# A hybrid decoder step on one Trainium2 core: w_o by halves with the sample tile first, and late experts placed on the chip

## What is computed

```python
h = x + merge_out(y_conv, y_nsa, gates, w_o)        # (g_a * y_conv + g_b * y_nsa) @ w_o
xf = rms_norm(h, g_ffn)
lg = xf @ w_rg + b_rg                               # 4 groups
le = (xf @ w_re + b_re).reshape(-1, 4, 8)           # 8 experts in each
g_star = argmax(lg); top_v, top_i = top_k(le[g_star], 2)
w_tok = softmax(top_v) * softmax(lg)[g_star]
eid = g_star * 8 + top_i
y = sum over the two experts of w_tok * (silu(xf @ w_gate[e]) * (xf @ w_up[e])) @ w_down[e]
out = rms_norm(h + y, g_final)
```

## Time and profile before

| what | us |
|---|---|
| median of 3 runs (821.12 to 822.25) | 821.67 |
| the profiled execution | 821.36 |
| its span | 819.5 |
| PE busy in the span | 772.4 (94%) |
| DVE / ACT / POOL busy | 371.3 / 199.9 / 170.7 |

### The profile page before, as it was taken

One profiled execution on the slowest core, in us unless ns is written; L12 is line 12 of the kernel. 1 busy time (PEld: TensorE's weight loads), 2 busy tenths in 40 slices (PEclk: granted clock), 3 DMA queues, 4 the chain that ended last, 5 costly groups with the idle time before them and its releaser, 6 DMA issues.

```text
span 819.5 us, 11726 instructions
## 1 busy us (share of the span) xinstructions
PE 772.4 (94%) x4589; PEld 540.2 (66%) x4589; DVE 371.3 (45%) x790; ACT 199.9 (24%) x435; POOL 170.7 (21%) x270
## 2 busy tenths in 40 slices
PE   5999999999999989999999999999999999998674
PEld 3657778878666667777767777774457855655431
DVE  2201999895488869103026632232137522232106
ACT  3000112131456651215226530000010112222114
POOL 2338548030000015000025220001000212232100
PEclk9999999999999999999999999999998999999878
DMA  9785545178000016521135359508007789999746
GB/s 310 173 30 189 157 104 149 45 218 281 2 1 2 1 32 177 180 77 52 51 85 162 117 148 319 215 1 290 31 26 286 283 325 412 408 403 386 310 158 242
DMA packets 91922, 140.05 MB, mean 171 GB/s; under 512 B 29909, under 2 KB 64881, under 8 KB 90703
## 3 DMA queue, kind: packets, MB, share of 16 engines
q1 hardware_dynamic: 75855, 102.46, 36.8%
q0 software_dynamic: 11392, 32.71, 13.8%
q10 hardware_dynamic: 4616, 4.08, 1.6%
HBM read 133.04 MB, written 21.14 MB: 188 GB/s over the span
## 4 chain that ended last, share of the span: by engine, by line
PE 85%; DVE 6%; DMA 5%; SPq 1%; issue 1%; ACT 1%; ACTq 0%; DVEq 0%; POOL 0%; POOLq 0%
PE ps L1925 18%; PE ps L2117 15%; PE ps L2457 7%; PE ps L2379 7%; PE ps L1949 5%; PE ps L2025 4%; PE ps L2473 3%; DMA arena<-w_up 2%; PE ps L2160 2%; PE ps L2135 2%; PE ps L2148 2%; PE ps L2447 2%; PE ps L2407 2%; DMA arena<-yscratch 2%; PE ps L2221 1%; PE ps L2003 1%
## 5 line engine op out<-in xcount | busy, mean ns | idle before, releaser
L2117 PE MATMUL ps<-xT,keep 128*128 128x288 f32 x512 | 126.9, 407 | 0.8 <-ACT h L1226 0.5
L2117 PEld LDWEIGHTS ps<-xT,keep 128*128 128x128 f32 x512 | 96.5, 190 | 27.4 <-ACT h L1226 0.9
L1925 PE MATMUL ps<-xT,arena 128*128 128x288 f32 x384 | 95.6, 408 | 1.1 <-DVE keep L1508 1.1
L1925 PEld LDWEIGHTS ps<-xT,arena 128*128 128x128 f32 x384 | 72.1, 190 | 20.7 <-issue 1.4
L1415 DVE SCALAR_TENSOR_TENSOR cv<-keep,cv 128x512 f32<-128x512 f32 x120 | 83.6, 746 | 1.4
L2379 PE MATMUL ps<-arena,xT 128*128 128x512 f32 x128 | 55.4, 592 | 0.0
L1000 POOL TENSOR_SCALAR keep<-keep,pmod 128x64 f32<-128x64 f32 x16 | 7.8, 508 | 176.2 <-PE ps L2160 120.0
L2379 PEld LDWEIGHTS ps<-arena,xT 128*128 128x128 f32 x128 | 24.2, 190 | 29.3 <-issue 29.2
L2457 PE MATMUL ps<-keep,mgT 128*64 128x256 f32 x224 | 41.7, 389 | 1.7 <-DMA mgT<-w_up 1.5
L1949 PE MATMUL ps<-mgT,xT 128*128 128x512 f32 (+1 forms) x128 | 43.3, 497 | 0.0
L1045 POOL DMA_INDIRECT yscratch<-cv,slots_of x19 | 19.0, 1001 | 100.2 <-PE ps L2447 67.2
(11 more groups left out here) (411 smaller groups left out, 1331.9 us busy)
## 6 DMA issues: line engine op xcount, KB each, us to landing
arena<-w_down SPq DMA_DIRECT2D x19, 512.0 KB, 16.2
keep<-w_in SPq DMA_DIRECT2D x16, 512.0 KB, 3.9
arena<-w_gate SPq DMA_DIRECT2D x15, 512.0 KB, 7.8
arena<-w_up SPq DMA_DIRECT2D x15, 512.0 KB, 10.8
keep<-w_gate SPq DMA_DIRECT2D x14, 512.0 KB, 10.1
keep<-w_up SPq DMA_DIRECT2D x14, 512.0 KB, 17.5
h<-x_prompt SPq DMA_DIRECT2D x8, 512.0 KB, 5.7
arena<-w_in SPq DMA_DIRECT2D x8, 512.0 KB, 8.7
```

The lines of the kernel that those rows point to most:

```text
L1925: last = mm(tokens(j)[:, b, :], weights(k), halves(x[:, k, :])[:, b, :], start=k == 0, stop=k == n_k - 1)
L2117: last = mm(out[:, 0:half], wmg[n // 2 % 3][:, k, :], xT[:, k, (n % 2) * half:(n % 2 + 1) * half], start=k == 0, stop=k == KD - 1, skip_gr ...
```

## The change

**w_o and router.** `w_o` is loaded as two halves of 512 output columns. The sample tile comes first, then the first half of the columns for tiles 0 to 3 (`wa`), then the second half (`wb`), tile by tile, with turn and logits of the tile before between its products. PE turns `h` itself, not the scaled tile; the scale is applied to the logits on DVE. ACT now writes the scaled tile to `xs2`. Fills are changed in number. When the first halves are done SP loads gate and up of positions 3 and 4; positions 7 and 8 now wait for the first two gathers.

**Late experts.** Positions from 11 on are no longer experts 11 to 31 in order. DVE works out a placing: experts with number 11 or more that have exactly one overflow block come first, from block 11 on, the others follow in order. The overflow blocks of the former are blocks 32, 33 and on, in the same order. The order of the pairs is now 0 to 6, 16, 7, 8, 9, 17, 10 to 15: 18 steps, with two pairs of overflow blocks as steps 7 and 11 (the eighth and the twelfth). The home of overflow block 32 + n is that of block 11 + n, so that its weights are there already; SP then loads nothing and raises the semaphores. Every block from 11 on is loaded by a number read from `eid`. DVE's weights on the identity (`diag`) move behind the first two `put_rows`.

```diff
-NUSUAL = NE // 2 + 3
-MID = 8
-STEPS = list(range(MID)) + list(range(NE // 2, NUSUAL)) + list(range(MID, NE // 2))
+NUSUAL = NE // 2 + 2
+AHEAD = 11
+STEPS = list(range(7)) + [16, 7, 8, 9, 17] + list(range(10, 16))
...
+        def home_w(x):
+
+            over = block_of(x) - NE
+            return (block_of(x) if over < 0 else AHEAD + over if x < 2 * NUSUAL else x) % HOMES_W
+
+        def in_home(x):
+            return [y for y in range(x) if home_w(y) == home_w(x)]
...
+            def placed(x):
+                at = sp.value_load(eid[0:1, 2 * N_OVER + x:2 * N_OVER + x + 1], min_val=0, max_val=NE - 1)
+                return None, bass.ds(at, 1)
+
             def freed(x, what):
-                take(sp, J_MOE + 4 * ((x - HOMES_W) // 2) + what)
-
-            more_of = {}
-
+                take(sp, J_MOE + 4 * (in_home(x)[-1] // 2) + what)
+
+            asked = {}
+
             def next_gate_up(x):
-                if blocks_of(x // 2) < NE // 2:
-                    freed(x, 1)
-                    gate_up(x)
-                    return
-                more_of[x] = used, e = over(x)
-                freed(x, 1)
+                asked[x] = used, e = over(x) if block_of(x) >= NE else placed(block_of(x))
+                freed(x, 1)
+                if used is None:
+                    gate_up(x, e)
+                    return
                 sp.nop(nofuse=True)
                 with sp.If(used < NE):
                     gate_up(x, e)
                 with sp.Else():
-                    sp.sem_inc(s_we[x % HOMES_W], 32)
+                    sp.sem_inc(s_we[home_w(x)], 32)
...
+            sp.wait_ge(s_eid, 3)
             for x in range(HOMES_W, 2 * NUSUAL):
-                if x == 2 * MID:
-                    sp.wait_ge(s_eid, 2)
                 next_gate_up(x)
                 if x - 2 >= HOMES_W:
                     next_down(x - 2)
...
-            merged_out(0)
-            merged_out(1)
-            normed_turned(0)
-            for i in range(2, NT):
-                merged_out(i)
-                logits(i - 2)
+            samples_merged_out()
+            merged_out(0, 0)
+            normed_turned(QT)
+            merged_out(0, 1)
+            logits(QT)
+            merged_out(0, 2)
+            merged_out(0, 3)
+            merged_out(1, 0)
+            for i in range(1, QT):
+                merged_out(1, i, 0, 2)
                 normed_turned(i - 1)
-            busy(JOB["lg", 3], 8)
-            logits(3)
-            normed_turned(4)
-            busy(JOB["lg", 4], 6)
-            logits(4)
-
-            busy(J_POS, 15)
+                merged_out(1, i, 2, 5)
+                logits(i - 1)
+                merged_out(1, i, 5, KD)
+            busy(JOB["n2", QT - 1], 10)
+            normed_turned(QT - 1)
+            busy(JOB["lg", QT - 1], 8)
+            logits(QT - 1)
+
+            busy(J_POS, 18)
             pe.wait_ge(s_chosen, QT)
...
-            busy(J_INV, 14)
```

More of the change, by code:

```diff
@@ L353, in build @@
         mt = cut(11072, 2, T)
-        wo = cut(0, KD, D)
+        wo = [cut(KD * 512 * n, KD, 512) for n in range(2)]
         xs2 = cut(0, NT, D, base=k1)
@@ L379, in build @@
         group_share, pair_share = room(NT), room(NT)
-        run, owners = room(NE + 1), room(N_OVER)
-        cv_flat = cv[:, :, :].rearrange("p a b -> p (a b)")
+        run, kept_run = room(NE + 1, where=KEPT_ROOM), room(NE + 1, where=KEPT_ROOM)
+        owners, missing, resident = (room(N_OVER, where=KEPT_ROOM) for n in range(3))
+        owner, ended = (room(N_OVER // 2, NE, where=KEPT_ROOM) for n in range(2))
         ye = [cut(1024 * s, D, base=cv_flat) for s in range(2)]
@@ L401, in build, with blocks_of @@
         so_far = room((NT + 1) * NE // 2).bitcast(BF16)
-        e_no, g_no, one_e, over_at = (room(NE) for n in range(4))
-        n_over = room(NE).bitcast(I32)
-        row_at, shift = room(2 * NT), room(NE)
+        e_no, n_over_words, shift, place64 = (room(NE, where=KEPT_ROOM) for n in range(4))
+        n_over = n_over_words.bitcast(I32)
+        g_no, one_e, over_at, kept, may_keep, late64, must_move, other_shift, moved = (room(NE) for n in range(9))
+        def blocks_of(p):
+            return STEPS[p] if p < NUSUAL else p
         WU = D
@@ L755, in _ @@
             sp.wait_ge(s_scat, 16 * NT)
+            for p in range(2):
+                sp.wait_ge(s_xe[p], 16)
             gate_up(7)
@@ L852, in scales_by_tile @@
         def scales_by_tile(pool, st, n):
-            for i in range(NT):
-                pool.wait_ge(s_sq, NT * n + i + 1)
+            for x, i in enumerate(LATE_TILES if n else range(NT)):
+                pool.wait_ge(s_sq, NT * n + x + 1)
                 c = slice(i, i + 1)
@@ L1836, in _ @@
             V.tensor_tensor(pair_exp, best[:, :, 1], best[:, :, 0], ALU.subtract).then_inc(s_sub, 1)
-            owner = grid.rearrange("p (n w) -> p n w", w=NE)
-            st.do(V.tensor_tensor(owner, run[:, 1:].unsqueeze(1).to_broadcast([P, N_OVER, NE]), blocks.unsqueeze(2).to_broadcast([P, N_OVER, NE]), ALU.is_le))
-            st.do(V.tensor_reduce(owners, owner, AX.X, ALU.add))
-            V.tensor_copy(eid[:, 0:N_OVER], owners).then_inc(s_eid, 1)
-            V.tensor_scalar(eid[:, N_OVER:], owners, float(NE - 1), None, ALU.min).then_inc(s_eid, 1)
+            late = NE - HOMES_W
@@ new lines, in _, with owners_of_blocks @@
+            st.do(V.tensor_tensor(expert_at, place64.unsqueeze(1).to_broadcast([P, late, NE]), e_row[:, HOMES_W:].unsqueeze(2).to_broadcast([P, late, NE]), ALU.is_equal))
+            st.do(V.tensor_tensor(expert_at, expert_at, e_no.unsqueeze(1).to_broadcast([P, late, NE]), ALU.mult))
+            st.do(V.tensor_reduce(moved[:, 0:late], expert_at, AX.X, ALU.add))
+            V.tensor_copy(eid[:, 2 * N_OVER + HOMES_W:], moved[:, 0:late]).then_inc(s_eid, 1)
+            def owners_of_blocks(st, n0, n1):
+                n, by_block = slice(n0, n1), lambda x: x.unsqueeze(1).to_broadcast([P, n1 - n0, NE])
+                number = blocks[:, n].unsqueeze(2).to_broadcast([P, n1 - n0, NE])
+                who, done = owner[:, 0:n1 - n0, :], ended[:, 0:n1 - n0, :]
+                st.mark(V.tensor_tensor(who, by_block(place64), number, ALU.is_le))
+                st.do(V.tensor_tensor(done, by_block(shift), number, ALU.is_le))
+                st.do(V.tensor_tensor(who, who, done, ALU.subtract))
+                st.do(V.tensor_tensor(who, who, by_block(e_no), ALU.mult))
+                st.do(V.tensor_reduce(owners[:, n], who, AX.X, ALU.add))
+                return V.tensor_copy(eid[:, N_OVER + n0:N_OVER + n1], owners[:, n])
```

260 lines of the change are left out of this document (151 added, 109 removed).

## The result

The changed kernel takes 829.88 us (median of 4 runs, 829.16 to 830.77), the kernel before 821.71 us on the same chip: a ratio of 1.0092, with a 95% interval of 1.0075 to 1.0108. The forecast was 826.0 with a range of 819.5 to 831.0, slower with a chance of 0.70: the direction held, and the time lies 3.9 us above the forecast. The profiled execution took 829.96 us, of which the span is 828.2, against 819.5.

The account below looks back on a forecast made before the run. The prediction took the expert weight stream to end last: restart 4.7, 48 loads 75.9, less 1.6, put the last up load at 782.4, 4.65 us later, so 821.36 + 4.65 = 826.0 us, range 819.5 to 831.

Parts of the forecast that it names:

- What bounds the kernel: Expert stage: the weight stream ends last; the last up load lands at 777.75, with 41.74 us left to the span's end.
- What is removed: Expert stage: one PE step of 6.47 us and nine loads, worth 14.2 us if the stream ran without a pause.
- rival (d): Late experts: no expert counts as kept, positions 14, 15 and 22 are fetched, with the waits: 840 us, chance 0.02.
- rival a: Weight stream: it doesn't pause, so the gain of 14.2 us comes: 807 us, chance 0.10.
- The hold: SP's queue: waits at 14 and 15 for steps 5 and 6 leave the stream nearly dry from about 669 to 694.5.
- Dry once more: SP's queue: after five loads from 694.5 to 702.5 the stream stops until position 18's gate load at 703.4.
- the forecast's restart: Weight stream after the third wait, from position 18's issue at 703.4: two loads take 4.7 us out of a dry stream.
- Step 0: First expert step, behind router, counting and slot work: taken as -0.2 us, bounds -2 and +7.4.
- rival (c): Before step 0: PE idles some 2.4 us, fills at clock 0.50 add 3.7 us: 829.7 us, chance 0.18.
- SP's resume: After step 6's down products: SP's branch and one expert-number reading, taken as 0.9 us (between 0 and 1.78).
- the tail: After the last up load: last products, scatter, reading back, final norm; 41.74 us, left alone by the change.
- Rival (b): Weight stream: the pause lets slow engines lose their backlog, landing at 777.6: 821.2 us, chance 0.20.

Follow-up runs that it names:

- e2_hold: Kernel before plus the three waits on SP's queue (positions 16, 17, down load of 15), same steps and loads: 835.86 us, ratio 1.0153.
- e10_list3_plain: Changed kernel with SP's loads reordered by when steps need them, without extra fills: 808.87 us, ratio 0.9828 to the kernel before.
- third list: SP's loads in the changed kernel ordered by need, nothing standing behind positions 14 and 15: 808.87 us alone, 809.32 with 64 fills.
- e4_third: Changed kernel with the down part of position 15 handled just ahead of position 22, moving the third wait: 830.15 us, ratio 1.0096.
- after_same: The changed kernel run again, nothing altered: 829.68 us, ratio 1.0098 to the kernel before.
- e3_fills: Changed kernel with 64 instead of 42 fills on PE ahead of the slot product: 828.44 us, ratio 1.0075 to the kernel before.
- e8_list3: Changed kernel with SP's loads ordered by need and 64 instead of 42 fills: 809.32 us, ratio 0.9843 to the kernel before.
- e5_fetch: Changed kernel, own order, with the nine loads of the three resident second blocks fetched all the same: 841.17 us, ratio 1.0248.
- first list: SP's loads in the changed kernel reordered: 16 to 21 and 24 before 14, 25 before 15: 815.73 us alone, 816.72 with 64 fills.
- second list: SP's loads in the changed kernel sorted by when homes come free: 828.41 us alone, 826.26 with 64 fills.

## Why the forecast held, and where it was off

**What bounds the kernel** was right: the weight stream, and in it SP's list. e2_hold shows the hold as a cause by itself; e10_list3_plain shows what the changed kernel gives without it.

**What is removed** was right: 97.74 MB on the load queue instead of 102.46, which is nine loads, so rival (d) is out. The forecast put their worth at 14.2 us in a stream without a pause, 807 (rival a). With the third list it is 14.1 us by the ratio 0.9828, but that the two agree is luck. What PE waited for in the kernel before, and then in e10_list3_plain, as far as it is up loads:

```profile
PE ps L2457 <- DMA keep<-w_up: 3.7, 1, 3.7
PE ps L2457 <- DMA arena<-w_up: 3.4, 2, 3.1
PE ps L2457 <- DMA mgT<-w_up: 1.5, 1, 1.5
```

```profile
PE ps L2535 <- DMA mgT<-w_up: 2.6, 1, 2.6
PE ps L2535 <- DMA keep<-w_up: 0.3, 1, 0.3
```

That is 8.6 us and 2.9. Together with one step of 6.47 us fewer and a step 0 that is 2.4 us later (655.28 for 652.86) it makes 9.8 us; the two profiled spans differ by 9.2 (819.5 and 810.3). So with the third list PE's own steps set most of the end, and the gain is a step and the waits that are gone, not nine times 1.58. The nine loads are not measured by themselves, and no run gave the kernel before a list by need: how much of the gain that list alone would bring there is open.

**The hold** was right in its place: gate waits of 14 and 15. Gain forgone and loss together were 14.2 + 4.65 = 18.9 us; 829.68 against 808.87 are 20.8, or 22 by the ratios, which for the same reason is no test of that sum. That GB/s would be near zero from 669 to 694 was wrong: from 668 to 690 4.06 MB are moved, but 2.86 of them are the gathers and scatters, which go on. The forecast's 353 GB/s beside it is the mean from 652 on; from 668 to 700 the kernel before moved 406.

**"Dry once more"** behind the third wait was wrong, and with it the moment from which the sum counted: e4_third shows that 18 could go out 4.3 us earlier for 1 us at most. The stream has restarted at 698.31. From there 54 loads land within 87.6 us, 1.62 each; the forecast's restart of 4.7 us for two loads and 48 at 1.58 less 1.6 came to 79.0 us, and 79.9 were measured from position 18 on. That the number held is luck: in place of the restart of 4.7 us stood the loads of positions 16 and 17, which were landing until 709.8, 3.8 us behind the issue of 18.

**Step 0** is the term that was mis-sized: -0.2 us taken, +2.0 measured. The count started at 634.20 (forecast 634.3), and the chain up to the slot product took 7.4 us (forecast 7.1). So far the forecast holds: the product is 0.4 us later than before. What failed is that rival (c)'s mechanism was left out of the term: it put PE's idle time at 2.4 us (2.80 measured) and asked whether the clock would be at 0.50 when the fills start. It was, for 3.4 us, and the fills took 1.6 us more; (c) had priced it at 3.7. The size is read from profiled executions (after_same has step 0 at 654.79, 0.04 from the first). Whether the whole time is shorter without that idle time, the times of e3_fills don't settle.

In the profiled execution the miss adds up: step 6's down products end at 705.01 instead of 702.54 (2.5 us, 2.2 of them from step 0), SP's resume takes 1.0 instead of 0.9, the stretch to the last landing 79.9 instead of 79.0, the tail 42.3 instead of 41.7. Together 4.0, less 0.1 outside the span (1.76 us instead of 1.86): the 3.9 us that the profiled execution's 829.96 lies above 826.0.

**Rival (b)** (an emptied backlog) is out by e2_hold, and in the changed kernel by the stretch from the issue of position 18 to the last landing: 79.9 us, where (b) has 74.2. The pace, on which it and the forecast differed, was 1.60 us a load from there, 1.62 from the restart.
The Trainium skill, "DMA: Bandwidth & Descriptors", section Bandwidth, has about 435 GB/s as the ceiling and about 358 as one core's part. With the list kept full, the runs show 397 to 408 over stretches of 32 and 48 us (e8_list3, e10_list3_plain): under the first and above the second, as before the change.

## What to carry over

A transfer list on one queue is a schedule: an entry that waits for a late home, even one with nothing to fetch, holds all entries behind it. Order such a list by need among what is free, and compare the time at which each entry's home comes free with that of its neighbours; neither position number nor time of release alone was good enough (829.9 and 828.4 against 809 us). Saved loads don't make up for a pause in the stream that they leave: fetching the nine all the same cost the changed kernel 11.5 us more (e5_fetch), yet without them it was slower than the kernel before until the pause was gone.

## What the runs showed of the hardware

- SP's issue of a load took 0.34 us behind a pause (698.31 in the changed kernel). In a stream that had been full for a while it often took 1.0 to 2.0 us, at times over 4 (4.66 at 706.09 in the kernel before): in the first list's run 1.43 and 1.81 us at 684.8 and 686.4, while 402 GB/s were moved. What SP should tell PE next comes late by it (2.5 us of PE at step 7).
- With a full queue an up load lands 16 to 19 us after its issue (16.03, 17.17, 18.39, 18.68), against at most 4.3 out of an empty one. Loads asked for early that aren't needed yet can delay by that much one that is (second list).
- In the second list's run PE waited 13.0 us for the load that landed at 764.98, and the granted clock was 0.50 (1.2 GHz) from 755.8 to 769.4, so the 32 products behind the wait took 5.78 us instead of 3.60: the wait cost 2.2 us more than itself. Behind the last holds of the kernel before and of the changed one they took 5.12 and 5.13. The Trainium skill, "TensorE: Matmul & The Clock Gate", section "HAM oscillation — how this bites in real kernels", tells of the same: work that starts after a wait for a transfer starts at the lower clock. The trace agrees here.
- After the same 2.80 us of idle time ahead of the slot product the lower clock lasted 3.4 us in the changed kernel's execution and 6.8 in those of the first and third list without fills, where the 66 fills took 9.9 and 10.1 us instead of 9.0.
